# A ring of six weight units in which the low part overwrites the raw weight, with splits four units ahead

## The chip, the cores and the metric

One core of a Trainium2 chip runs one program: a transformer block with a mixed retention and neighbourhood attention, followed by two layers of a second kind of block. The metric is the device time of one execution in microseconds (us). Five engines take part: TensorE (PE) multiplies, VectorE (DVE) and ScalarE (ACT) do elementwise work, GpSimd (POOL) mostly issues DMAs, and the sync engine (SP) issues the DMAs of the weights. Each engine runs its instructions in order and waits on semaphores.

## The reference

```
x = x + 0.5 * rms(swiglu(rms(x) @ w_in) @ w_out)           # ffn1: 1024 -> 2 x 2816 -> 1024
x = x + rms(token_mixing(rms(x)))                          # w_mix_in 1024 x 6656, retention, attention, gates
x = x + 0.5 * rms(swiglu(...))                             # ffn2
mod = silu(c) @ ada_w + ada_b                              # 2 layers x 6 vectors of 1024
for i in range(2):                                         # layer 0: MoBA attention, layer 1: differential
    x = layer_norm(alpha * x + (1 + gate1) * attention(x * (1 + scale1) + shift1))
    x = layer_norm(alpha * x + (1 + gate2) * (relu(h @ w_up) ** 2) @ w_down)   # h = x * (1 + scale2) + shift2
```

There are 256 tokens of 1024 features, all in float32. The weights are read once, 198 MiB of them, so every weight is used for 256 tokens only.

## The kernel before

**Units.** All weights pass through a ring in units of 1 MiB, a tile of 128 x 2048 float32. There are 198 units (`N_UNITS`), numbered in the order in which PE uses them; unit u lies in slot u % `RING`. PE multiplies in the one-pass float32r format, and to keep precision each weight is split: ACT writes `hi_w`, the weight rounded to float32r (`split_hi`, L782), and DVE writes `lo_w = w_raw - hi_w` (`split_lo`, L1089). For each product PE then does three matmuls, hi x hi, lo x hi and hi x lo (`three`, L384 to L386), 24 matmuls of 512 columns in a unit. Activations are split alike into `xT_hi`, `xT_lo`, `hT_hi` and `hT_lo`.

**What sets the order.** SP issues the requests for units in order. Ahead of unit u it waits for `w_lo`, that is for the lo split of unit u - 4, which is the last reader of the raw slot (`slot_free`). ACT waits for the landing of unit u, and for PE to have used unit u - 4 (`w_used`), the last reader of `hi_w` and `lo_w` in that slot. DVE waits for `w_hi`. PE waits for `w_lo` ahead of a unit (`in_unit`, `down_unit`) and counts `w_used` after it. The splits are written into the programs of ACT and DVE by hand, between their other work, `AHEAD` = 3 units ahead of the unit that PE has in the same step.

**Start.** ACT and DVE split unit 0, then the first activations, then units 1 to `AHEAD` - 1 in a loop. After the loop ACT forms the squares of x (`x_squares`, L824) and `c_act` (L909), and DVE the factor of the norm (`x_factor`, L1119 to L1128), which the first SwiGLU activation needs. POOL waits for `w_lo` to reach `AHEAD` and then starts to fetch the weights of the adaLN modulation.

**SwiGLU blocks.** `swiglu` runs 11 blocks of 3 units: two units of gate and up projections, one of the down projection. PE does the gate and up units of block i + 1, transposing the hidden tile of block i between them (L429), then waits for `hT_lo` and does the down unit of block i. ACT has the activation (L840) and `hT_hi` (L847) between its splits, DVE the product (L1226) and `hT_lo` (L1183). In 8 of the 11 blocks of each SwiGLU, and in the first MLP, DVE also multiplies a piece of the adaLN weights by `c_act` (`piece_half` twice, four operations of L1194 and L1197 each, and `piece_fold`). A piece is two transfers of 1 MiB, one for each half, into a single buffer; POOL asks for each half of the next piece when DVE is through with that half (L1651). In block 1 of the first SwiGLU DVE has some 25 tiny operations more (`small_vectors`).

**Later stages.** The mixing stage, the two attentions and the two MLPs take units through the same ring. Between two stages PE waits while ACT and DVE form a norm.

Of the kernel before, what the change touches and what calls it, by code (L numbers as in the profile page):

```python
# [11 lines left out]
F32R = mybir.dt.float32r  # L12
# [3 lines left out]
P = 128  # L16
# [9 lines left out]
MLP_B = 512  # L26
N_MLP = D_MLP // MLP_B
UNIT = 2048
RING = 4
AHEAD = 3  # L30
RET_H, RET_DK, RET_DV = 4, 128, 256
NA_H, NA_D = 8, 64
GRID = 64
# [67 lines left out]
def ring_slot(u):  # L101
    return u % RING


def landed(u):
    return 32 * (u // RING + 1)

# [15 lines left out]
def two_blocks_kernel(nc, d, out):  # L123
    with ExitStack() as ctx:
        def sb(name, shape, dt=F32):
            return ctx.enter_context(nc.sbuf_tensor(name, shape, dt))

        def sem(name):
            return ctx.enter_context(nc.semaphore(name))


        w_raw = sb("w_raw", [P, RING, UNIT])
        hi_w = sb("hi_w", [P, RING, UNIT], F32R)
        lo_w = sb("lo_w", [P, RING, UNIT], F32R)
        x = sb("x", [P, NT, D])
        xT_hi = sb("xT_hi", [P, KD, SEQ], F32R)
        xT_lo = sb("xT_lo", [P, KD, SEQ], F32R)
# [92 lines left out]

        w_landed = [sem(f"w_landed{i}") for i in range(RING)]
        w_hi, w_lo, w_used = sem("w_hi"), sem("w_lo"), sem("w_used")
# [40 lines left out]
        def _(sp):  # L273
            def slot_free(u):

                if u >= RING:
                    sp.wait_ge(w_lo, u + 1 - RING)

            def unit(u, src, k):
                slot_free(u)  # L280
                dst = w_raw[:, ring_slot(u), :].rearrange("p (k n) -> p k n", k=k)
                sp.dma_start(dst, src).then_inc(w_landed[ring_slot(u)], 32)

            def swiglu_in(u, w, i, half):
                slot_free(u)
                dst = w_raw[:, ring_slot(u), :].rearrange("p (k g f) -> p k g f", k=4, g=2)
                for g in range(2):
                    src = w[:, 4 * half:4 * half + 4, g, i * FF_B:(i + 1) * FF_B]
                    sp.dma_start(dst[:, :, g, :], src).then_inc(w_landed[ring_slot(u)], 16)

            def swiglu(u0, w_in, w_out):
                w_in = w_in.rearrange("(k p) (g f) -> p k g f", p=P, g=2)
                w_out = w_out.rearrange("(b k p) n -> p b k n", p=P, k=2)

                def out_unit(u, i):
                    slot_free(u)
                    dst = w_raw[:, ring_slot(u), :].rearrange("p (k n) -> p k n", k=2)
                    src = w_out[:, i:i + 1, :, :].rearrange("p b k n -> p (b k) n")
                    sp.dma_start(dst, src).then_inc(w_landed[ring_slot(u)], 32)

                def step(u, i):
                    swiglu_in(u, w_in, i + 1, 0)
                    swiglu_in(u + 1, w_in, i + 1, 1)
                    out_unit(u + 2, i)

                swiglu_in(u0, w_in, 0, 0)
                swiglu_in(u0 + 1, w_in, 0, 1)
                for i in range(N_FF - 1):
                    step(u0 + 2 + 3 * i, i)
                out_unit(u0 + 3 * N_FF - 1, N_FF - 1)  # L310
# [46 lines left out]
            u = U_MIX + 2 * N_MIX  # L357
# [416 lines left out]
        def _(act):  # L774
            def split_hi(u):

                if u >= N_UNITS:
                    return
                act.wait_ge(w_landed[ring_slot(u)], landed(u))
                if u >= RING:  # L780
                    act.wait_ge(w_used, u + 1 - RING)
                act.activation(hi_w[:, ring_slot(u), :], w_raw[:, ring_slot(u), :], ACT.Copy).then_inc(w_hi, 1)  # L782

            def chunk_his(first, n, off, dst, dst0, scale=None):
# [48 lines left out]
            def swiglu(u0, b0, n, between=None):  # L833
                def activation(b, i):
                    act.wait_ge(w_used, u0 + 2 if i == 0 else u0 + 4 + 3 * (i - 1))
                    if i >= 1:
                        act.wait_ge(hid_done, b)
                    for t in range(NT):
                        pair = 4 + 2 * (i % 2)
                        ins = act.activation(act_s[:, t, 0:FF_B], ps[:, (pair + t) * BANK:(pair + t) * BANK + FF_B],  # L840
                                             ACT.Silu, scale=rstd_x[:, t:t + 1])
                    ins.then_inc(act_done, 1)

                def hidden_hi(b, i):
                    act.wait_ge(hidT, b + 1)
                    off = (4 + 2 * (i % 2)) * BANK
                    act.activation(hT_hi[:, 0:2, :], ps[:, off:off + 2 * SEQ].rearrange("p (c n) -> p c n", c=2),  # L847
                                   ACT.Copy).then_inc(hidT_hi, 1)

                split_hi(u0 + AHEAD)  # L850
                act.wait_ge(rstd_x_done, n)
                split_hi(u0 + AHEAD + 1)
                activation(b0, 0)
                for i in range(N_FF - 1):
                    u, b = u0 + 2 + 3 * i, b0 + i
                    split_hi(u + AHEAD)
                    hidden_hi(b, i)
                    split_hi(u + AHEAD + 1)
                    activation(b + 1, i + 1)
                    split_hi(u + AHEAD + 2)  # L860
                    if i == 1 and between is not None:
                        between()
                hidden_hi(b0 + N_FF - 1, N_FF - 1)
                split_hi(u0 + 3 * N_FF - 1 + AHEAD)

# [74 lines left out]
            u = U_MIX  # L940
# [830 lines left out]
```

## Time and profile before

| what | us |
|---|---|
| median of 3 runs | 1383.76 (1381.53 to 1384.84) |
| the profiled execution | 1381.94 |
| its span, first to last instruction | 1380.1 |
| PE busy | 1252.5 (91%) |
| DVE busy | 966.0 (70%) |
| ACT busy | 596.2 (43%) |
| POOL busy | 122.0 (9%) |

The span is what the trace covers; 1.8 us of the profiled execution's own time lie outside it. The profiled execution is 1.82 us quicker than the median of the three runs. Busy time counts an engine's instructions; matmuls overlap one another, so a busy PE is not PE at its peak. All times in the rows below count from the first instruction. The core moved 274.31 MB by DMA, of which 209.80 MB went through SP's queue and 63.56 MB through POOL's. The mean granted clock of TensorE was 0.954 of full speed.

### The profile page before, as it was taken

The numbers are of one execution on the slowest core, as the hardware profiler recorded it, in microseconds if no ns is written. First come the engines' busy times: TensorE is split into PE (matmuls) and PEld (weight loads), VectorE is DVE, ScalarE is ACT, GpSimd is POOL, SyncE is SP. The second block draws the span as 40 slices with busy tenths as digits, with TensorE's granted clock in tenths as the row PEclk, the third lists the DMA queues.
The fourth block names the chain that finished last, engine by engine and source line by source line (L and its number), as shares of the span: only waits on it lengthen the run. The fifth ranks groups of instructions, "written<-read, shape, count | busy, mean of one in ns | idle before, by whom it ended". The sixth has DMA issues, their size and how long they took to land.

```text
span 1380.1 us, 14621 instructions
## 1 busy us (share of the span) xinstructions
PE 1252.5 (91%) x5776; PEld 1027.9 (74%) x5776; DVE 966.0 (70%) x1244; ACT 596.2 (43%) x722; POOL 122.0 (9%) x148
## 2 busy tenths in 40 slices
PE   6999998999999899998899869999949975899995
PEld 5888876887888688887677647888738754688884
DVE  5998847765566698884756488878776876745454
ACT  5444444446653444444355334444334552434340
POOL 2000220004200000000000030001030001200000
PEclk9999998999999999999899789999979987999998
DMA  9989973535455599974543238787715330555520
GB/s 308 373 297 325 289 245 115 190 132 174 138 183 183 198 314 316 313 245 152 179 152 122 76 112 305 283 292 268 263 60 202 123 122 30 198 184 182 190 85 31
DMA packets 132596, 274.31 MB, mean 199 GB/s; under 512 B 6176, under 2 KB 51440, under 8 KB 132528
## 3 DMA queue, kind: packets, MB, share of 16 engines
q1 hardware_dynamic: 114672, 209.80, 44.5%
q0 software_dynamic: 17792, 63.56, 13.7%
q8 instruction: 46, 0.75, 0.2%
q14 instruction: 22, 0.18, 0.0%
q10 hardware_dynamic: 64, 0.02, 0.0%
HBM read 270.41 MB, written 2.93 MB: 198 GB/s over the span
## 4 chain that ended last, share of the span: by engine, by line
PE 77%; DVE 14%; ACT 3%; issue 3%; DMA 2%; SPq 0%; POOL 0%; DVEq 0%; ACTq 0%
PE ps L384 24%; PE ps L386 23%; PE ps L385 23%; PE ps L429 3%; DVE lo_w L1089 2%; DVE xT_lo L1110 1%; DMA w_raw<-in_ffn_w_in 1%; DVE piece_acc L1197 1%; DMA aux<-in_ada_w 1%; ACT area L1025 1%; DVE area L1517 1%; DVE xT_hi L1109 1%; PE ps L580 1%; DVE area L1142 1%; DVE x L1144 1%
## 5 line engine op out<-in xcount | busy, mean ns | idle before, releaser
L1089 DVE TENSOR_TENSOR lo_w<-w_raw,hi_w 128x2048 fp32r<-128x2048 f32 x198 | 454.3, 2300 | 175.1 <-ACT hi_w L782 174.7
L384 PE MATMUL ps<-hi_w,xT_hi 128*128 128x512 f32 x1120 | 453.0, 404 | 35.3 <-DVE xT_lo L1110 12.9
L782 ACT ACTIVATE hi_w<-w_raw 128x2048 fp32r<-128x2048 f32 x198 | 378.6, 1913 | 214.3 <-PE ps L386 203.1
L385 PE MATMUL ps<-hi_w,xT_lo 128*128 128x512 f32 x1120 | 442.2, 395 | 0.0
L386 PE MATMUL ps<-lo_w,xT_hi 128*128 128x512 f32 x1120 | 442.1, 395 | 0.0
L384 PEld LDWEIGHTS ps<-hi_w,xT_hi 128*128 128x128 f32 x1120 | 214.3, 191 | 85.2 <-issue 23.4
L386 PEld LDWEIGHTS ps<-lo_w,xT_hi 128*128 128x128 f32 x1120 | 213.9, 191 | 46.5
L385 PEld LDWEIGHTS ps<-hi_w,xT_lo 128*128 128x128 f32 x1120 | 214.8, 192 | 42.5
L384 PE MATMUL ps<-hi_w,hT_hi 128*128 128x512 f32 x464 | 182.2, 393 | 9.0 <-DVE hT_lo L1183 9.0
L386 PE MATMUL ps<-lo_w,hT_hi 128*128 128x512 f32 x464 | 181.2, 391 | 0.0
L385 PE MATMUL ps<-hi_w,hT_lo 128*128 128x512 f32 x464 | 181.2, 391 | 0.0
L384 PEld LDWEIGHTS ps<-hi_w,hT_hi 128*128 128x128 f32 x464 | 87.5, 189 | 28.8 <-DVE hT_lo L1183 10.9
L386 PEld LDWEIGHTS ps<-lo_w,hT_hi 128*128 128x128 f32 x464 | 87.5, 189 | 18.3
L385 PEld LDWEIGHTS ps<-hi_w,hT_lo 128*128 128x128 f32 x464 | 87.6, 189 | 18.0
L429 PE MATMUL ps<-ident,area 128*128 128x128 f32 x432 | 64.1, 295 | 31.6 <-ACT area L806 23.0
L429 PEld LDWEIGHTS ps<-ident,area 128*128 128x128 f32 x432 | 56.0, 153 | 42.0 <-ACT area L806 24.2
L1197 DVE SCALAR_TENSOR_TENSOR piece_acc<-aux,c_act,piece_acc 128x512 f32<-128x512 f32 x112 | 84.1, 751 | 4.1 <-DMA aux<-in_ada_w 0.6
L1183 DVE TENSOR_TENSOR hT_lo<-ps,hT_hi 128x512 fp32r<-128x512 f32 (+1 forms) x38 | 34.7, 913 | 58.1 <-ACT hT_hi L879 46.1
L847 ACT ACTIVATE hT_hi<-ps 128x512 fp32r<-128x512 f32 x22 | 13.2, 598 | 80.8 <-PE ps L429 80.8
L879 ACT ACTIVATE hT_hi<-ps 128x1024 fp32r<-128x1024 f32 x16 | 16.4, 1026 | 72.4 <-PE ps L429 72.4
L1025 ACT ACTIVATE area<-area,top 128x128 f32<-128x128 f32 x64 | 28.4, 444 | 40.3 <-DVE top L1521 30.4
L1651 POOL DMA_DIRECT2D aux<-in_ada_w x32 | 24.0, 750 | 237.2 <-DVE piece_acc L1197 206.2
(208 smaller groups left out, 912.9 us busy)
## 6 DMA issues: line engine op xcount, KB each, us to landing
w_raw<-in_ffn_w_in SPq DMA_DIRECT2D x88, 512.0 KB
aux<-in_ada_w POOLq DMA_DIRECT2D x32, 1024.0 KB, 7.2
w_raw<-in_mlp_w_up SPq DMA_DIRECT2D x32, 1024.0 KB
w_raw<-in_mlp_w_down SPq DMA_DIRECT2D x32, 1024.0 KB
w_raw<-in_w_mix_in SPq DMA_DIRECT2D x26, 1024.0 KB
w_raw<-in_ffn_w_out SPq DMA_DIRECT2D x22, 1024.0 KB
area<-in_ada_w POOLq DMA_DIRECT2D x16, 1024.0 KB, 5.7
w_raw<-in_moba_w_in SPq DMA_DIRECT2D x12, 1024.0 KB
```

The costliest lines, as they stand in the source:

```text
L384: pe.matmul(dst, lhs_hi, rhs_hi, start=start, stop=False)
L385: pe.matmul(dst, lhs_lo, rhs_hi, start=False, stop=False)
L386: return pe.matmul(dst, lhs_hi, rhs_lo, start=False, stop=stop)
L429: mm = pe.transpose(ps[:, off:off + P], src[:, t, col0 + c * P:col0 + (c + 1) * P], ident[:, :])
L580: mm = pe.matmul(ps[:, off:off + SEQ], nqT[row, h // 2, t * P:(t + 1) * P], nkT[row, h // 2, :], start=True, stop=True)
L782: act.activation(hi_w[:, ring_slot(u), :], w_raw[:, ring_slot(u), :], ACT.Copy).then_inc(w_hi, 1)
L879: act.activation(hT_hi[:, :, :], bank(pair, 2).rearrange("p (c n) -> p c n", c=4), ACT.Copy).then_inc(hidT_hi, 1)
L1025: ins = act.activation(pr, pr, ACT.Exp, bias=top[:, e, t:t + 1], accum_out=total[:, c % 2, 2 * e + t:2 * e + t + 1])
L1089: vec.tensor_tensor(lo_w[:, ring_slot(u), :], w_raw[:, ring_slot(u), :], hi_w[:, ring_slot(u), :].bitcast(F32), ALU.subtract).then_inc(w_l ...
L1183: vec.tensor_tensor(hT_lo[:, 0:chunks, :], src.rearrange("p (c n) -> p c n", c=chunks), hT_hi[:, 0:chunks, :].bitcast(F32), ALU.subtract). ...
L1197: ins = vec.scalar_tensor_tensor(out=acc, in0=row, scalar=c_act[:, c:c + 1], in1=acc, op0=ALU.mult, op1=ALU.add)
L1651: pool.dma_start(dst, ada[layer][:, 4 * half:4 * half + 4, i * BANK:(i + 1) * BANK])\
```

## The change

The ring becomes six units of two tensors instead of four units of three. `lo_w` is placed on the bytes of `w_raw`, so DVE's subtraction writes over its first operand. A raw slot is then in use until PE has used the unit, so SP waits for `w_used` of unit u - 6 ahead of its request for unit u. ACT's own wait for `w_used` goes, since a landed unit implies it. `AHEAD` is 4: each split in the programs of ACT and DVE is that of one unit later, the loops at the start hold unit 3 too, and POOL's first wait is for four lo splits.

```diff
-RING = 4
-AHEAD = 3
+RING = 6
+AHEAD = 4
...
+        w_base = (nc.sbuf_base + 31) // 32 * 32
         w_raw = sb("w_raw", [P, RING, UNIT])
+        lo_w = nc.alloc_sbuf_tensor_at("lo_w", [P, RING, UNIT], F32R, offset=w_base)
         hi_w = sb("hi_w", [P, RING, UNIT], F32R)
-        lo_w = sb("lo_w", [P, RING, UNIT], F32R)
...
             def slot_free(u):
                 if u >= RING:
-                    sp.wait_ge(w_lo, u + 1 - RING)
+                    sp.wait_ge(w_used, u + 1 - RING)
...
                 act.wait_ge(w_landed[ring_slot(u)], landed(u))
-                if u >= RING:
-                    act.wait_ge(w_used, u + 1 - RING)
                 act.activation(hi_w[:, ring_slot(u), :], w_raw[:, ring_slot(u), :], ACT.Copy).then_inc(w_hi, 1)
```

## Rows read from the trace of the kernel before

**Rows 1.** PE's waits: who waited for whom, us in total, times, longest.
```profile
PE ps L445 <- DVE x L1144: 18.7, 6, 5.8
PE ps L384 <- DVE hT_lo L1183: 9.0, 6, 2.4
```

**Rows 2.** The waits of ACT and DVE, and of SP's queue, same columns.
```profile
ACT hi_w L782 <- PE ps L386: 203.1, 63, 8.1
DVE lo_w L1089 <- ACT hi_w L782: 174.7, 96, 13.4
ACT hi_w L782 <- DMA w_raw<-in_ffn_w_in: 9.8, 3, 7.8
...
SPq L282 <- DVE lo_w L1089: 902.9, 132, 32.2
```

**Rows 3.** DVE's groups by shape: count | busy us, mean ns | idle before, releaser.
```profile
L1089 DVE TENSOR_TENSOR lo_w<-w_raw,hi_w 128x2048 fp32r<-128x2048 f32 x198 | 454.3, 2300 | 175.1 <-ACT hi_w L782 174.7
...
L1258 DVE TENSOR_TENSOR area<-area 128x1024 f32<-128x1024 f32 x16 | 19.6, 1223 | 13.8 <-ACT area L873 13.8
...
L1413 DVE TENSOR_TENSOR area<-area 128x1024 f32<-128x1024 f32 x2 | 2.5, 1226 | 0.0
```

**Rows 4.** The chain that ended last, first 80 us: start, us, what.
```profile
23.72 2.30 DVE lo_w L1089
...
26.30 0.76 POOL aux L1651
27.06 13.60 DMA aux<-in_ada_w
...
76.41 0.50 PE ps L384
```

**Rows 5.** Timeline of ACT at the start: start, us, operation [idle before <-releaser].
```profile
21.76 1.92 ACT L782 ACTIVATE hi_w<-w_raw 128x2048 fp32r<-128x2048 f32 x1 [0.78 <-DMA w_raw<-in_ffn_w_in]
23.59 1.04 ACT L824 ACTIVATE area<-x 128x1024 f32<-128x1024 f32 x1
...
27.19 3.71 ACT L782 ACTIVATE hi_w<-w_raw 128x2048 fp32r<-128x2048 f32 x2
30.80 0.81 ACT L840 ACTIVATE area<-ps,rstd_x 128x256 f32<-128x256 f32 x2
```

**Rows 6.** Timeline of DVE at the start.
```profile
33.61 0.87 DVE L1226 SCALAR_TENSOR_TENSOR area<-ps,rstd_x,area 128x256 f32<-128x256 f32 x2
...
39.35 0.68 DVE L1183 TENSOR_TENSOR hT_lo<-ps,hT_hi 128x512 fp32r<-128x512 f32 x1
40.68 3.12 DVE L1197 SCALAR_TENSOR_TENSOR piece_acc<-aux,c_act,piece_acc 128x512 f32<-128x512 f32 x4 [0.65 <-DMA aux<-in_ada_w]
```

**Rows 7.** Timelines of PE, ACT and DVE: first block, then a settled one.
```profile
36.02 0.60 PE L429 MATMUL ps<-ident,area 128*128 128x128 f32 x4
...
149.46 1.92 ACT L782 ACTIVATE hi_w<-w_raw 128x2048 fp32r<-128x2048 f32 x1 [2.85 <-PE ps L386]
...
166.25 1.92 ACT L782 ACTIVATE hi_w<-w_raw 128x2048 fp32r<-128x2048 f32 x1 [2.85 <-PE ps L386]
...
151.41 2.29 DVE L1089 TENSOR_TENSOR lo_w<-w_raw,hi_w 128x2048 fp32r<-128x2048 f32 x1 [1.61 <-ACT hi_w L782]
...
156.38 0.69 DVE L1183 TENSOR_TENSOR hT_lo<-ps,hT_hi 128x512 fp32r<-128x512 f32 x1
...
160.55 0.39 PE L384 MATMUL ps<-hi_w,hT_hi 128*128 128x512 f32 x1
```

**Rows 8.** Transfers: issues with median to landing, stretches (last columns PEclk, DMA, GB/s).
```profile
aux<-in_ada_w POOLq DMA_DIRECT2D x32, 1024.0 KB, 7.2
...
30.00:80.00 50.00, 49.30 (x224) 40.49 (x223) 47.52 (x71) 25.27 (x25) 4.07 (x6) 1.00 0.96 340
...
1225.39 5.85 SPq L282 DMA_DIRECT2D w_raw<-in_mlp_w_up  x2
...
1230.00:1231.00 1.00, 1.00 (x6) 0.85 (x5) 0.82 (x1) 0.00 (x0) 0.00 (x0) 1.00 0.02 8
```

## Prediction

> **What bounds the kernel now.** I read first what TensorE waited for. Its longest waits are for the norm of a finished stage, 18.7 us in 6 waits, with others of that kind; inside the stages it waits for the split hidden tile, `hT_lo`, 9.0 us in 6 waits [rows 1]. No wait of TensorE names `lo_w` or `hi_w`: it never waits for a weight unit after the first. Next the engines that prepare units. ACT idles 203.1 us ahead of `hi_w` because PE has not given a slot back, and 9.8 us for a landing; DVE idles 174.7 us for `hi_w`; the SP queue stands 902.9 us at L282 for `lo_w` [rows 2]. These are long, but they are the waits of engines that are ahead of the bound engine. So outside the boundaries and the attention chains the bound is PE's own work, and a deeper split lead can't pay there.
>
> One stretch is different. The chain of waits, cut to the first 80 us, is not PE's until 76.41: it goes from unit 2's lo split (23.72) to POOL's issue of the first adaLN pieces (26.30), through that transfer (27.06, 13.60 us), to the second piece half on DVE (40.68), and then along DVE until `hT_lo` releases PE at 76.41 [rows 4, 6]. Whatever enters this chain enters the time of the kernel. Everything after 76.41 is shifted with it.
>
> **The change, part by part.** The bytes of SBUF stay: 3 tensors of 4 units become 2 of 6. No matmul, split or transfer is added or removed (198 of each split [rows 3]).
>
> In place: DVE's 198 subtractions now write over their first operand. The trace has a same-size pair to compare, both 128x1024 f32: out of place (L1258) 1223 ns, in place (L1413) 1226 ns [rows 3]. That is 3 ns in 1223, at most 6 ns each on the 2300 ns of a split, 1.2 us in all on DVE, which is idle ahead of these splits 175.1 us [rows 3]. A gain has no reason, since shape and types are unchanged. I take 0. If the cover were gone it would be 1.2 us.
>
> ACT's dropped wait on `w_used`: the same release now stands in front of the request on SP. In the quiet up-and-down stage ACT was held by PE; now it is held by a landing. A request at 1225.39 has moved its bytes by 1230 (the window 1230 to 1231 moves 8 GB/s) [rows 8], so a landing takes about 5 us. The split in a given place of ACT's order is now that of the next unit, and its request leaves one unit earlier than ACT's old release: a PE unit is (166.25 - 149.46)/3 = 5.6 us, the same place of ACT's order three units apart [rows 7]. So the landing comes 5.6 - 5 = 0.6 us ahead of the old release. ACT gains up to 0.6 us that nobody waits for: 0. SP's wait on `w_used` has only later weight requests and the final store queued behind it; what a late landing does hold is ACT's next instruction, the hidden tile's `hT_hi`, and this is priced next.
>
> The loaded SwiGLU blocks: pieces of 1 MiB share the DMAs there, and the median of such a piece is 7.2 us [rows 8]; unit landings are not listed, so I take that row for them. Between 5 and 13.60 us [rows 4, 8] the 7.2 is nearest, being the same size in the same stage. The new place of 149.46 has its request at 143.9 and its landing at 151.1, 1.6 us late. DVE's lo split moves from 151.41 to 153.0, the four piece operations behind it likewise, and `hT_lo` from 156.38 (0.69 us long) to 158.0, ending at 158.7. PE takes it at 160.55 [rows 7]: 1.9 us of cover left. DVE's gap of 1.61 us ahead of its split takes the lateness up, so it does not grow from block to block. Cost 0; if the cover is gone, each us of landing beyond about 9.1 us is a us per block.
>
> The preamble is where AHEAD costs. Both `for u in range(1, AHEAD)` loops, ACT's and DVE's, now hold unit 3 as well, ahead of `x_squares` and `x_factor`; and `pool.wait_ge(w_lo, AHEAD)` now waits for unit 3's lo split. Unit 2 landed at 21.74 (ACT took it at 21.76 out of a wait for the DMA) [rows 5]; the requests are in one queue and the rate of the first full stretch is 340 GB/s [rows 8], so 1 MiB more is 3.1 us: unit 3 lands near 24.8. Then:
> - ACT: hi of unit 3 from 24.8 to 26.7, where `x_squares` began at 23.59 [rows 5]. Two squares, a table load and `c_act`, 3.6 us as before (23.59 to 27.19), end at 30.3; hi of units 4 and 5 end at 34.1; `activation` of block 0 starts there and not at 30.80. That is +3.3.
> - DVE: lo of unit 3 ends at 26.7 + 2.3 = 29.0, where lo of unit 2 ended at 26.0. `x_factor` ends near 31.0, lo of units 4 and 5 run from 32.3 to 36.8, and the product that began at 33.61 [rows 6] begins near 36.7: +3.1. PE reaches the transposes that need it at 36.02 [rows 7] and the product ends near 37.5, so PE stands 1.5 us. This is inside the delay below, not on top.
> - The next lo split, 4 piece operations and `hT_lo` follow; `hT_lo` was at 39.35 [rows 6] and comes at 42.4, ending at 43.1. PE is due there near 43.4. No stall.
> - POOL: its issue moves from 26.30 to 29.3, +3.0. The transfer took 13.60 us [rows 4], so the second half lands at 43.7 instead of 40.66. DVE is free for it at 43.1 (it used to stand 0.65 us for it [rows 6]).
>
> So DVE starts the second half between 2.4 us (its own order) and 3.0 us (landing) later. Nothing from there to 76.41 is idle except waits of well under a us, so PE resumes at 76.41 + 2.4 to 3.0. Could the next landings add? The unit whose split follows block 0 is requested when PE ends unit 3 (near 43.6) and needs to be in ACT's hands by about 51; at 7.2 us it is just there, at 8.4 us it adds 1.2: upper end 4.2. Below: if unit 3 landed with unit 2, hi would start at 23.7 and all is 1.1 us less: lower end 1.3.
>
> Which of 2.4 and 3.0? The row shows 13.60 us for 2 MiB behind the weights. The Trainium skill (DMA: Bandwidth & Descriptors, Queues, rings and completion order) says that a DMA engine takes the queue rows with work in turn, a packet of each. By that rule POOL's pieces get about half the rate however many weight requests stand in the other queue, so the transfer keeps its length when it starts later, and the result is the 3.0; if it were bytes in order of request, the same bytes would be through at 40.66 as before and DVE's own order would leave 2.4. Without the page I take the row's length unchanged: 3.0.
>
> The split lead inside the stages: one more unit split per unit of PE lead, same counts in each slot. The chain at the boundaries holds norms and chunk splits, no landing. Behind POOL's longer first wait stand only the pieces and later loads, whose other events are as before. 0. In the last stage one split fewer trails: nothing waits for it.
>
> **Sum.** Profiled run 1381.94 + 3.0 = 1384.9. That run is 1.8 below the median of the three, 1383.76; against the median 1386.8.
>
> **The rivals.**
> - *Start delay hidden* (0.22): the landing of unit 3 and of the pieces is quicker than bytes over rate, or requests of units 4 and 5 that leave earlier fill it. Then 0 to 2 us: 1384.8. For: units 4 and 5 no longer wait for lo splits. Against: the chain is DVE's work, which this does not shorten.
> - *Faster* (0.08): ACT freed of its 203.1 us [rows 2] hands over the in-stage tiles sooner and takes away part of PE's `hT_lo` waits, 9.0 us [rows 1]. Of these the ones at ends of stages are chains behind the last matmul, so about 3 us can go: 1380.8. Against: those tiles wait for PE's transposes, not for ACT.
> - *Slower by landings* (0.15): a six-slot ring asks for a unit only when PE has finished the sixth before it, where the old one asked after a lo split some 7 units ahead of PE. If loaded landings take over 9.1 us, each SwiGLU block with pieces stalls; at 10 us it is 0.9 us in 16 blocks, 14 us, with the start 1401. For: 13.60 for two pieces. Against: the 7.2 median. The Trainium skill (same page, Rules for kernel authors) advises to issue a DMA early and wait late; this change does the reverse for the raw units, and this rival is what the rule would cost here.
> - That the lead does nothing at all is no case of its own: it is the forecast without its 3.0, the first rival.
>
> **How the numbers follow.** Forecast 0.55. A measurement of this kernel tells about 0.2% (2.8 us) from no change. The forecast straddles that line: 1386.8 is 3.0 above, its ends 1.3 and 4.2; with about 1 us of spread in medians I give 0.37 of its 0.55 to slower, 0.18 to same. The first rival is all same, the second 0.07 faster and 0.01 same, the third slower. Slower 0.52, same 0.41, faster 0.07. Range: from 1383.0 (most of the hidden case in) to 1391.5 (the upper end, spread, and the mild cases of the landing rival); left out are the gain and the heavy landing cases.
>
> **What would show it.** In the changed profile: three splits become four ahead of the squares on ACT; the squares start near 26.6; POOL's first piece issue near 29.3; the product near 36.7; a PE wait of about 1.5 us near 37; the `hT_lo` wait at about 79 instead of 76.41. SP's waits name PE, no longer DVE; ACT's waits ahead of `hi_w` name DMA and are no shorter in sum than about 150 us; SwiGLU blocks still take 16.8 us. Blocks over 17 us, or PE waits on `lo_w`, would prove the landing rival; a missing shift of POOL's issue would prove the forecast wrong.

## The result and the profile after

The changed kernel takes 1399.05 us in the median (1396.28 to 1405.92, 4 runs), the kernel before 1383.66 (1381.53 to 1384.84, 4 runs): a ratio of 1.012, 95% interval 1.0081 to 1.016. By the ratio it is slower by some 16.6 us (0.012 x 1383.66; the two medians differ by 15.4), where 3.0 were forecast; the time lies beyond the range. The changed kernel scatters over 9.6 us in its 4 runs, the kernel before over 3.3 in these 4 and over 6.1 in 27 on another chip.

The profiled execution of the changed kernel has a span of 1398.4 us, 18.3 more than before. From its page come the busy times of the engines (us, share, instructions), the groups of the two splits (count | busy us, mean ns | idle before, releaser), and the transfers of the adaLN pieces (size, median us to landing; it was 7.2 [rows 8]):

```profile
PE 1258.1 (90%) x5776; PEld 1029.5 (74%) x5776; DVE 964.9 (69%) x1244; ACT 596.7 (43%) x722; POOL 123.0 (9%) x148
...
L1088 DVE TENSOR_TENSOR lo_w<-w_raw,hi_w 128x2048 fp32r<-128x2048 f32 x198 | 452.4, 2293 | 189.6 <-ACT hi_w L781 189.2
...
L781 ACT ACTIVATE hi_w<-w_raw 128x2048 fp32r<-128x2048 f32 x198 | 377.9, 1914 | 236.1 <-DMA w_raw<-in_ffn_w_in 103.2
...
aux<-in_ada_w POOLq DMA_DIRECT2D x32, 1024.0 KB, 7.7
```

The waits, the lines that answer to [rows 1, 2] (us in total, times, longest):

```profile
ACT hi_w L781 <- DMA w_raw<-in_ffn_w_in: 103.2, 22, 11.8
...
ACT hi_w L781 <- DMA w_raw<-in_mlp_w_down: 39.5, 15, 4.7
...
ACT hi_w L781 <- DMA w_raw<-in_mlp_w_up: 39.1, 10, 4.5
...
PE ps L385 <- DVE hT_lo L1182: 19.3, 10, 2.8
...
SPq L283 <- PE ps L387: 910.0, 132, 28.6
SPq L290 <- PE ps L387: 205.1, 39, 15.2
```

Three things are to be seen. First, the in-place split costs nothing: 2293 ns against 2300. Second, ACT's idle time ahead of `hi_w` is no shorter than before, 236.1 us against 214 (203.1 for PE and 9.8 for landings [rows 2]), and 234.6 of it are now waits for landings. Third, PE's waits for `hT_lo` went from 9.0 us in 6 [rows 1] to 19.3 us in 10. The 18.3 us divide so: 10.3 are these waits, 0.5 is a new wait for the first product, 0.7 the first transfer of x, which released PE at 7.20 instead of 6.52 (nothing that the change touches), and 5.6 are busy time of PE, 1258.1 against 1252.5 for the same 5776 matmuls. About 1.2 are spread over small gaps.

PE's busy time can grow only if matmuls get slower. The windows behind the new waits show it (columns as in [rows 8]: the granted clock PEclk is third from the end):

```profile
80.00:90.00 10.00, 10.00 (x39) 8.06 (x38) 9.86 (x11) 1.98 (x2) 0.75 (x1) 0.83 0.94 327
...
510.00:520.00 10.00, 8.17 (x37) 6.44 (x36) 9.79 (x11) 5.95 (x5) 1.50 (x2) 1.00 0.77 255
550.00:560.00 10.00, 8.57 (x31) 6.90 (x32) 9.84 (x12) 3.83 (x2) 1.50 (x2) 0.83 1.00 320
```

In both stretches of 0.83 PE ran some 3.4 us at 1.2 GHz in place of 2.4, which costs some 1.7 us each (0.17 x 10), 3.4 of the 5.6 us. The same stretch of the kernel before, 80 to 90, has 1.00. The other 2.2 us were not placed; the clock also falls at the ends of stages, in both kernels and not by the same amount. The 5.6 is itself rough: in the profiled executions of ring6_ahead3, ring6_ahead2, before_start4 and before_small_pieces (below), all within 0.1% of the kernel before, PE is busy for 1254.0, 1252.4, 1251.5 and 1251.0 us.

**One late landing, followed.** The chain of waits from 496 to 516, in the second SwiGLU (start, us, what):

```profile
496.83 10.52 DMA w_raw<-in_ffn_w_in
...
507.38 1.93 ACT hi_w L781
...
509.32 2.29 DVE lo_w L1088
511.62 0.41 DVE piece_acc L1193
...
512.05 0.76 DVE piece_acc L1196
...
512.84 0.76 DVE piece_acc L1196
...
513.62 0.75 DVE piece_acc L1196
514.37 0.61 DVE hT_lo L1182
...
515.03 0.50 PE ps L385
```

A landing releases ACT, ACT DVE, DVE does four piece operations and then `hT_lo`, and PE has been standing for it. The timelines give both ends of the landing. SP's queue and ACT, here and one such place later:

```profile
496.42 1.00 SPq L290 DMA_DIRECT2D w_raw<-in_ffn_w_in  x2
...
507.38 1.92 ACT L781 ACTIVATE hi_w<-w_raw 128x2048 fp32r<-128x2048 f32 x1 [8.30 <-DMA w_raw<-in_ffn_w_in]
...
532.15 1.57 SPq L290 DMA_DIRECT2D w_raw<-in_ffn_w_in  x2
...
543.77 1.92 ACT L781 ACTIVATE hi_w<-w_raw 128x2048 fp32r<-128x2048 f32 x1 [8.97 <-DMA w_raw<-in_ffn_w_in]
```

The units took 11.0 and 11.6 us from the first request to ACT. PE then waited 1.83 us at 515.03 and 2.50 us at 551.43. Take the 9.1 us at which the prediction put the end of the cover, that is the time that a landing may take before PE has to wait: 11.0 - 9.1 = 1.9 and 11.6 - 9.1 = 2.5. This limit was right to a tenth of a us; the landings were not 7.2.

The wait of 2.53 us at 185.25 has a longer landing behind it, and a longer cover. The chain there:

```profile
165.90 0.37 SPq L290
166.31 14.03 DMA w_raw<-in_ffn_w_in
180.36 1.93 ACT hi_w L781
182.31 2.29 DVE lo_w L1088
184.60 0.61 DVE hT_lo L1182
```

This block has no piece, so the four piece operations, 2.8 us at 511.62 above, do not stand between `lo_w` and `hT_lo`. From the request to ACT it is 14.5 us, and 14.5 - 9.1 - 2.8 = 2.6.

### The profile page after: what moved, and what is told of

Read it like the earlier page. It is cut to its first block, busy times and chain, and to the rows that moved or that the text cites. A ratio compares the mean times of both kernels' runs of the same rounds, so it can differ in the third digit from the quotient of the medians.

```text
span 1398.4 us, 14429 instructions
## 1 busy us (share of the span) xinstructions
PE 1258.1 (90%) x5776; PEld 1029.5 (74%) x5776; DVE 964.9 (69%) x1244; ACT 596.7 (43%) x722; POOL 123.0 (9%) x148
## 4 chain that ended last, share of the span: by engine, by line
PE 71%; DVE 15%; DMA 5%; ACT 4%; issue 3%; SPq 1%; DVEq 0%; ACTq 0%
PE ps L385 22%; PE ps L387 21%; PE ps L386 21%; DMA w_raw<-in_ffn_w_in 4%; PE ps L430 3%; DVE lo_w L1088 2%; DVE piece_acc L1196 2%; ACT hi_w L781 1%; DVE xT_lo L1109 1%; SPq L290 1%; ACT area L1024 1%; DVE area L1516 1%; DVE xT_hi L1108 1%; DMA w_raw<-in_diff_w_in 1%; PE ps L581 1%
## 5 line engine op out<-in xcount | busy, mean ns | idle before, releaser
L1088 DVE TENSOR_TENSOR lo_w<-w_raw,hi_w 128x2048 fp32r<-128x2048 f32 x198 | 452.4, 2293 | 189.6 <-ACT hi_w L781 189.2
L781 ACT ACTIVATE hi_w<-w_raw 128x2048 fp32r<-128x2048 f32 x198 | 377.9, 1914 | 236.1 <-DMA w_raw<-in_ffn_w_in 103.2
L385 PE MATMUL ps<-hi_w,hT_hi 128*128 128x512 f32 x464 | 184.9, 398 | 19.3 <-DVE hT_lo L1182 19.3
L386 PEld LDWEIGHTS ps<-hi_w,hT_lo 128*128 128x128 f32 x464 | 88.8, 191 | 18.3
L1196 DVE SCALAR_TENSOR_TENSOR piece_acc<-area,c_act,piece_acc 128x512 f32<-128x512 f32 x56 | 42.1, 751 | 1.8
```

The costliest lines, as they stand in the source:

```text
L385: pe.matmul(dst, lhs_hi, rhs_hi, start=start, stop=False)
L386: pe.matmul(dst, lhs_lo, rhs_hi, start=False, stop=False)
L1088: vec.tensor_tensor(lo_w[:, ring_slot(u), :], w_raw[:, ring_slot(u), :], hi_w[:, ring_slot(u), :].bitcast(F32), ALU.subtract).then_inc(w_l ...
L1196: ins = vec.scalar_tensor_tensor(out=acc, in0=row, scalar=c_act[:, c:c + 1], in1=acc, op0=ALU.mult, op1=ALU.add)
```

## The experiments

The theory: a request leaves when PE has finished unit u - RING, and the split of unit u stands where PE takes up unit u - AHEAD. Between them lie RING - AHEAD - 1 units of 5.6 us, called the distance here: 5.6 us in the changed kernel. A landing may take that and the slack of ACT and DVE, 9.1 us in all in a block with a piece. Most do not take more, but those beside two adaLN transfers of 1 MiB, or beside the bias table, sometimes do. A low granted clock follows some of the waits. The rivals: the in-place split or the new waits themselves cost the time; the deeper start costs more than 3 us; the low clock is chance.

Each ratio is against the kernel before on the same chip, with its 95% interval. The medians of the kernel before there were 1383.41 us (27 runs) for ring6_ahead3, before_start4 and the two with small pieces, 1383.09 (11 runs) for after_late_split, ring5_ahead3, ahead5 and after_small_late_table, and 1384.08 (17 runs) for the other four.

**ring6_ahead3**, the changed kernel with the old lead:

```diff
 RING = 6
-AHEAD = 4
+AHEAD = 3
```

> The changed kernel with AHEAD back at 3: ring of six, low part in place, SP waiting for PE, but each split is that of the unit three ahead. Theory (landings): a unit is requested when PE ends the sixth before it, and with AHEAD 3 its split stands one unit later in the orders of ACT and DVE, 5.6 us later, so even the landings of 10 to 12 us seen in the changed kernel come in time. And the loops at the start have three units again, so the start costs nothing. I expect 1383 to 1385, within 2 us of the kernel before. Rival (the ring itself costs, by the subtraction in place or by requests that follow PE): some 10 us or more of the 15 us stay, 1393 or higher.

Measured: 1383.57 us, ratio 0.999 (0.9981 to 0.9999). The ring of six, the split in place and the moved waits cost nothing together; all of the 16.6 us hangs on AHEAD. PE's wait of 0.70 us at 76.41 is gone too, and ACT's idle time ahead of its splits shrinks to 43.6 us. Long landings are still there; they are covered. Beside the bias table a unit that was requested at 156.30 reached ACT 17.3 us later, and PE waits for no `hT_lo` between 76 and 203:

```profile
156.30 11.80 SPq L290 DMA_DIRECT2D w_raw<-in_ffn_w_in  x4
...
173.65 1.92 ACT L781 ACTIVATE hi_w<-w_raw 128x2048 fp32r<-128x2048 f32 x1 [8.78 <-DMA w_raw<-in_ffn_w_in]
```

Here is ACT's group (columns as in [rows 3]), and below it those of three more kernels of the series:

```profile
L781 ACT ACTIVATE hi_w<-w_raw 128x2048 fp32r<-128x2048 f32 x198 | 373.5, 1913 | 43.6 <-DMA w_raw<-in_ffn_w_in 23.1 <-DMA w_raw<-in_mlp_w_down 9.1 <-DMA w_raw<-in_w_mix_out 7.1
```

ring6_ahead2:

```profile
L781 ACT ACTIVATE hi_w<-w_raw 128x2048 fp32r<-128x2048 f32 x198 | 371.7, 1914 | 15.4 <-DMA w_raw<-in_ffn_w_in 8.4 <-DMA w_raw<-in_ffn_w_out 4.1 <-DMA w_raw<-in_w_mix_out 1.6
```

ring5_ahead3:

```profile
L781 ACT ACTIVATE hi_w<-w_raw 128x2048 fp32r<-128x2048 f32 x198 | 377.9, 1915 | 243.4 <-DMA w_raw<-in_ffn_w_in 130.9 <-DMA w_raw<-in_mlp_w_down 77.7 <-DMA w_raw<-in_w_mix_out 8.6
```

ahead5:

```profile
L781 ACT ACTIVATE hi_w<-w_raw 128x2048 fp32r<-128x2048 f32 x198 | 379.0, 1914 | 639.3 <-DMA w_raw<-in_ffn_w_in 135.9 <-DMA w_raw<-in_ffn_w_out 123.1 <-DMA w_raw<-in_mlp_w_down 108.3
```

**ring5_ahead3**, a shorter ring and the old lead, the same distance as in the changed kernel:

```diff
-RING = 6
-AHEAD = 4
+RING = 5
+AHEAD = 3
```

> The changed kernel with a ring of five and splits three ahead. Theory: what decides is RING minus AHEAD, the units that PE uses up between a request and the place of its split in ACT's order; it is 2 here as in the changed kernel and 3 in ring6_ahead3. So PE's waits for the hidden tile in the loaded blocks are there again, some 9 to 13 us, while the start costs nothing: 1392 to 1397. Rival (a split lead of four is what hurts, by the order of work on DVE): within 2 us of the kernel before, since the lead is three.

Measured: 1397.14 us, ratio 1.0099 (1.0084 to 1.0114), as slow as the changed kernel although no split is added to its start. PE's waits for `hT_lo` sum to 19.9 us in 11; the longest, 2.90 us, does stand in the start, at 46.71, behind a unit that the shorter ring requests later. Not the lead and not the ring but their difference decides.

**ahead5**, the distance of nothing:

```diff
 RING = 6
-AHEAD = 4
+AHEAD = 5
```

> The changed kernel with splits five ahead in the ring of six. A split then stands one PE unit, 5.6 us, behind its request, and a quiet landing takes 5 us behind a request that itself comes late. Theory (RING minus AHEAD): now even landings of 7 us come late by 5 to 7 us in ACT's order, ahead of the hidden tile; each loaded SwiGLU block loses 2 to 4 us and the quiet ones little: 1425 to 1470. Rival (only rare late landings of over 10 us matter): 1405 to 1415.

Measured: 1492.13 us, ratio 1.0797 (1.0771 to 1.0822). The direction holds; the loss is beyond what was expected. Far more of each landing is now met, so ACT idles 639.3 us ahead of its splits, PE waits 56.7 us in 21 for `hT_lo`, and its busy time is 1292.1, 39.6 more than before. These two make 87 of the 109 us of the span; the others were not followed.

**ring6_ahead2**, a distance of three units, 16.8 us:

```diff
 RING = 6
-AHEAD = 4
+AHEAD = 2
```

> The changed kernel with a lead of two: a request leaves four units before its split. By the theory (only RING minus AHEAD counts, and three is enough) it is level with ring6_ahead3 and with the kernel before, within 0.1%, since two units of lead, 11 us, still cover ACT's and DVE's splits, 1.9 and 2.3 us. Rival (the splits need the lead of three against the work that ACT and DVE do at once at the ends of stages): PE waits for lo_w there, 5 to 20 us slower.

Measured: 1382.73 us, ratio 0.9994 (0.9984 to 1.0004). Even a lead of two units is enough, and a distance of more than two units brings nothing more. The series is then:

| RING, AHEAD | distance | ratio | ACT idle ahead of `hi_w` | PE's waits for `hT_lo` |
|---|---|---|---|---|
| 6, 2 | 16.8 us | 0.9994 | 15.4 | 8.3, 5 times |
| 6, 3 | 11.2 | 0.999 | 43.6 | 8.3, 5 |
| 5, 3 | 5.6 | 1.0099 | 243.4 | 19.9, 11 |
| 6, 4 (the change) | 5.6 | 1.012 | 236.1 | 19.3, 10 |
| 6, 5 | 0 | 1.0797 | 639.3 | 56.7, 21 |

**before_start4**, the start alone, put into the kernel before:

```diff
-                split_hi(u0 + AHEAD)
+                if u0 != U_FFN1:
+                    split_hi(u0 + AHEAD)
...
-            for u in range(1, AHEAD):
+            for u in range(1, 4):
                 split_hi(u)
...
-            pool.wait_ge(w_lo, AHEAD)
+            pool.wait_ge(w_lo, 4)
```

> The kernel before with one thing of the change: unit 3 is split in the loops ahead of the squares and of the norm's factor, and POOL's first wait is for four low splits. Ring of four, and from block 0 on the splits are three ahead as before. Theory (the start is a term of its own): DVE's chain to the first hidden tile that PE waits for is 2.4 to 3.2 us later, 1386 to 1387. In this kernel unit 3's split leaves its old place, so DVE's total work up to there is the same and only the order differs: if the cost is one more split of 2.3 us in DVE's busy chain, it is nearly 0 here; if it is the later start of the pieces' transfer and of the squares, it is up to 3.

Measured: 1385.04 us, ratio 1.0007 (0.9999 to 1.0016), 1.0 us more (-0.1 to 2.2). PE's wait that stood at 76.41 stands at 78.00:

```profile
78.00 0.50 PE L384 MATMUL ps<-hi_w,hT_hi 128*128 128x512 f32 x1 [1.57 <-DVE hT_lo L1184]
```

So in the old ring the start costs 1.0 us by the ratio and 1.6 by the place of this wait, not 3.0. Its requests at the start are not those of the changed kernel, and unit 3's split is only moved here, not followed by one more, so this does not settle what the start costs there.

**after_late_split**, the changed kernel with the extra split taken out of the start and put behind unit 13:

```diff
             def split_hi(u):
+                if u in (3, 14):
+                    return split_hi_of(13) or split_hi_of(14) if u == 14 else None
+                split_hi_of(u - 1 if 3 < u < 14 else u)
+
+            def split_hi_of(u):
...
-            pool.wait_ge(w_lo, AHEAD)
+            pool.wait_ge(w_lo, 3)
```

> The changed kernel, but up to block 3 of the first SwiGLU the splits are three ahead as before: the loops at the start hold units 1 and 2, POOL's first wait is for three low splits, and the one extra split is made behind that of unit 13. From there all is as in the changed kernel. Theory (the start and the landings are two terms that add): the wait near 77 shrinks to 0.7 us or less, 2.4 to 3.2 us go, with the stretch of low clock behind it up to 4.8; the waits at 180, 510, 550, 620 and 1005 stay. 1394 to 1397. Rival (the start's delay is made up later, or the landing waits come from where it shifted the pieces): 1399 as the changed kernel, or below 1390.

Measured: 1393.48 us, ratio 1.0077 (1.0062 to 1.0092). Some 6 of the 16.6 us go, and some 10 stay; the intervals of this kernel and of the changed one overlap a little, so the 6 is rough. In its profile the squares begin at 24.20, and the wait near 76 is 0.88 us long where the changed kernel has 2.21 at 79.61. With the 0.51 at 37 that is 1.8 us; another 1.7 are the low clock of 80 to 90, which is 1.00 here. The wait in the last blocks of the first SwiGLU is there still, 3.89 us at 182.09. What was expected of the second SwiGLU did not come: from there on the kernel is the changed one, and yet the waits of 1.83, 2.50 and 1.28 us are 0.23 us at 562.27 and 0.67 us at 613.67 in this execution, and 550 to 560 runs at 1.00. So not all of the 6 us can be put down to the start, and how late the landings are changes from one execution to another.

**after_small_pieces** and **before_small_pieces** take the bytes away from beside the units: of all adaLN pieces but the first of each group of eight only 64 of 512 columns are fetched. The modulation that comes of it is therefore not that of the reference; every instruction of the engines stays.

```diff
-                        pool.dma_start(dst, ada[layer][:, 4 * half:4 * half + 4, i * BANK:(i + 1) * BANK])\
+                        w = BANK if p == p0 else 64
+                        pool.dma_start(dst[:, :, 0:w], ada[layer][:, 4 * half:4 * half + 4, i * BANK:i * BANK + w])\
                             .then_inc(mod_landed[half], 16)
```

> The changed kernel, but of the adaLN pieces only the first of each group of eight is fetched whole; of the others only 64 of 512 columns are, 128 KB instead of 1 MiB a half, so the modulation is not computed rightly. DVE's operations stay the same. Theory (landings are late because pieces share the DMAs): a unit's landing stays near 5 us, the waits of PE for the hidden tile at 185, 515, 551, 621 and 1008 go, and with them the three stretches of lower granted clock that follow two of them; what is left is the start. 1385 to 1388, 2 to 4 above the next kernel. Rival (the stalls are from the order of ACT and DVE, not from DMA traffic): still 10 us or more above it.

> The kernel before with the same cut of the pieces' transfers, for comparison with the one above; the modulation is not computed rightly. It did not wait for landings after the first 40 us, so it stays at 1382 to 1384; up to 1 us may go at the start, where DVE stood 0.65 us for a piece.

Measured: 1392.49 us, ratio 1.0061 (1.0046 to 1.0077), and for the kernel before 1383.51, ratio 0.9999 (0.9988 to 1.0009). The pieces' bytes cost the kernel before nothing. The waits of the changed kernel at 515, 551 and 621 are gone without them: those landings were late because of the pieces. (In after_late_split they had nearly gone with the pieces whole, so pieces beside a unit make a late landing possible and not certain.) The time is above the 1385 to 1388 that were expected, for one wait remains, and it is longer than the one at 185 in the changed kernel:

```profile
187.33 0.80 PE L385 MATMUL ps<-hi_w,hT_hi 128*128 128x512 f32 x1 [7.36 <-DVE hT_lo L1182]
```

There POOL moves the table of the attention bias, after the last piece of the first SwiGLU. In the changed kernel the timelines of POOL and ACT show the transfer, and the landing beside it:

```profile
160.68 1.67 POOL L1664 DMA_DIRECT2D rel_scratch<-area  x1 [5.55 <-DMA area<-in_na_rel_bias]
178.26 0.55 POOL L1638 DMA_DIRECT2D aux<-in_mix_post_norm  x1 [15.91 <-DMA rel_scratch<-area]
...
180.36 1.92 ACT L781 ACTIVATE hi_w<-w_raw 128x2048 fp32r<-128x2048 f32 x1 [11.81 <-DMA w_raw<-in_ffn_w_in]
```

**after_small_late_table** is after_small_pieces with these transfers moved behind the first SwiGLU, and **after_late_table** is the changed kernel with that move alone:

```diff
-            pool.wait_ge(rel_zero, 1)
...
-            pool.wait_ge(rel_out, 16)
...
             pool.dma_start(rot1.rearrange("p c t n -> p (c t n)"), d["rot1"]).then_inc(ld_tab, 16)
+            pool.wait_ge(norm_done[1], S_FFN1 + 1)
+            pool.wait_ge(rel_zero, 1)
...
+            pool.wait_ge(rel_out, 16)
```

> after_small_pieces with one more edit: POOL's transfer of the bias table (1792 KB) and its loads wait for the end of the first SwiGLU. Of the pieces but the first of each eight only 64 of 512 columns are fetched, so the modulation is not computed rightly. Theory (landings are late because of what shares the DMAs, and in after_small_pieces the table's transfer made the one wait of 7.36 us at 187 and the lower clock behind it): those 10 us go and the start is left, 1384.5 to 1387. Rival (the wait at 187 is from the order of DVE's work in block 8): it stays, 1392.

> The changed kernel with the bias-table transfer of POOL moved behind the first SwiGLU, and nothing else. Theory (the table's transfer made the landing of 14 us at unit 30): the wait of 2.5 us near 185 goes, the waits in the second SwiGLU stay, and moving the table costs about 2 us in the mixing stage: 1395 to 1400, the same as the changed kernel within 0.3%. Rival (late landings come whatever else is on the DMAs there): a wait of over 2 us near 185 stays.

Measured: 1388.77 us, ratio 1.0044 (1.0031 to 1.0057), and 1396.23, ratio 1.009 (1.0069 to 1.0111). In both the wait near 185 is gone. In the second the waits of the second SwiGLU are there as before, 1.47, 3.14 and 1.09 us at 518, 555 and 625. In the first PE waits for `hT_lo` only 8.3 us in 5, as in ring6_ahead3: with the pieces small and the table later, PE waits for no late landing any more, and 6 of the 16.6 us are left. Somewhat more than expected; of these, some 4 are there by the end of the first SwiGLU (its last `hT_lo` wait at 205.48 against 201.61 in the kernel before), and the table itself makes PE wait some 2 us in the mixing stage. These 4 us are the nearest to a price of the start in the changed kernel's own ring, and they are not exact either: the first 50 us differ between executions of like programs. The granted clock is 0.96 and 0.87 from 30 to 50 here, worth some 1.6 us, and 0.76 from 20 to 30 in ring6_ahead3, where the profiled executions of the changed kernel and of the kernel before have 1.00. And the wait that the changed kernel has at 79.61 stands at 82.63 in after_late_table, whose start is the same program.

**stall_long** and **stall_short** measure what a wait costs beyond itself. They are ring6_ahead3 with 13 and 10 empty operations on DVE ahead of `hT_lo` in four blocks:

```diff
+                    if i in (3, 8):
+                        if piece is not None:
+                            vec.wait_ge(mod_step, KD * piece + 4)
+                        vec.wait_ge(hidT_hi, b + 1)
+                        for _ in range(13):
+                            then(vec.tensor_scalar(piece_acc[:, 0, :], piece_acc[:, 0, :], 1.0, None, ALU.mult))
                     hidden_lo(b, i, 2)
```

> The kernel before with a ring of six and a lead of three (level with before), and 13 empty operations on DVE, 0.51 us each as the 0.48 us multiplies of the pieces, ahead of hT_lo in 4 of the 22 SwiGLU blocks (blocks 3 and 8 of each SwiGLU). The cover there is 4.0 us, so PE should wait 4 times about 2.6 us, 10.4 us in all. Theory (a wait of 2.2 us or more is followed by a stretch of low granted clock, which costs again): the time grows by more than the waits, 13 to 17 us, and some of the four stretches behind a wait show a granted clock of 0.83. Rival (the low clock in the changed kernel came by chance, as it does in the kernel before): the time grows by the waits alone, 10 to 11 us.

> The same with 10 operations instead of 13: PE should wait 4 times about 1.1 us, 4.4 us in all. Theory: such short waits leave the granted clock at 1.00, the time grows by 4 to 5 us. Rival (each wait costs the clock something, however short): 6 us or more.

Measured: 1403.82 us, ratio 1.0142 (1.0129 to 1.0155), and 1396.28, ratio 1.0093 (1.0078 to 1.0107). The waits did not come out equal. PE's timeline of stall_long:

```profile
98.36 0.50 PE L385 MATMUL ps<-hi_w,hT_hi 128*128 128x512 f32 x1 [4.08 <-DVE hT_lo L1182]
189.84 0.80 PE L385 MATMUL ps<-hi_w,hT_hi 128*128 128x512 f32 x1 [5.57 <-DVE hT_lo L1182]
555.61 0.50 PE L385 MATMUL ps<-hi_w,hT_hi 128*128 128x512 f32 x1 [2.02 <-DVE hT_lo L1182]
643.50 0.50 PE L385 MATMUL ps<-hi_w,hT_hi 128*128 128x512 f32 x1 [1.93 <-DVE hT_lo L1182]
```

They sum to 13.6 us; stall_short has 2.82, 3.30, 0.63 and 0.54, together 7.3. The times grew by 0.0142 x 1384.08 = 19.7 us (17.9 to 21.5) and 12.9 us (10.8 to 14.8), 6 us more than these sums. But the waits are known in the profiled execution alone, and it was the quickest of each kernel. Taken by itself it is 1401.56 - 1384.08 = 17.5 and 1393.02 - 1384.08 = 8.9 us slower, so 3.9 and 1.6 us beyond its own waits. The other executions may have waited longer. That more than the waits is lost is borne out by the clock. Windows of stall_long:

```profile
100.00:110.00 10.00, 10.00 (x40) 8.16 (x39) 9.93 (x10) 0.00 (x0) 0.75 (x1) 0.86 0.59 212
...
190.00:200.00 10.00, 10.00 (x34) 8.06 (x35) 8.27 (x5) 1.91 (x1) 5.35 (x5) 0.76 0.38 107
550.00:560.00 10.00, 7.99 (x28) 6.10 (x28) 9.52 (x17) 5.01 (x5) 0.75 (x1) 0.84 0.84 287
640.00:650.00 10.00, 8.07 (x36) 6.33 (x36) 9.79 (x12) 4.44 (x4) 0.00 (x0) 1.00 0.34 107
```

The clock fell behind 4.08, 5.57 and 2.02 us and not behind 1.93. Windows of stall_short:

```profile
90.00:100.00 10.00, 7.18 (x28) 5.46 (x27) 9.50 (x17) 4.82 (x5) 1.44 (x2) 0.88 0.88 287
...
180.00:190.00 10.00, 6.70 (x23) 5.06 (x22) 9.65 (x16) 4.31 (x5) 0.85 (x1) 0.83 0.97 307
540.00:550.00 10.00, 9.37 (x44) 7.44 (x43) 7.87 (x16) 3.81 (x5) 0.75 (x1) 1.00 0.78 274
```

It fell behind 2.82 and 3.30 and not behind 0.63. The border that the theory drew at 2.2 us is not sharp: ring5_ahead3 has 0.83 from 120 to 130 behind a wait of 1.80 at 118.64, the changed kernel 1.00 behind one of 2.53 at 185.25. In ahead5 it is 1.00 behind one of 3.06 at 645.85. Nor is the low clock mere chance: in the profiled executions of the kernel before and of the four kernels level with it no stretch of 10 us between 50 and 200 or between 490 and 640 is below 1.00. What short waits alone would cost stays open, since two of the four were long.

## Why the prediction was wrong

The direction was right, the size was not; the mechanism that decides was named as the third rival, with a chance of 0.15 and a price of 14 us. The step that failed is the term for the loaded SwiGLU blocks, set at 0.

**In place, the dropped wait on ACT, the ring itself: 0.** Right. The split takes 2293 ns against 2300, and ring6_ahead3 is level with the kernel before.

**The start: +3.0.** Right in its places. The squares began at 26.71 (26.6 foretold), POOL's first piece was issued at 29.43 (29.3), the product began at 36.73 (36.7), PE waited for it near 37 (0.51 us, where 1.5 was foretold), and the wait for `hT_lo` stood at 79.61, 3.20 after 76.41 (about 79). From DVE's timeline of the changed kernel:

```profile
36.73 0.87 DVE L1225 SCALAR_TENSOR_TENSOR area<-ps,rstd_x,area 128x256 f32<-128x256 f32 x2
...
42.48 0.68 DVE L1182 TENSOR_TENSOR hT_lo<-ps,hT_hi 128x512 fp32r<-128x512 f32 x1
43.08 3.11 DVE L1196 SCALAR_TENSOR_TENSOR piece_acc<-aux,c_act,piece_acc 128x512 f32<-128x512 f32 x4
...
53.44 2.29 DVE L1088 TENSOR_TENSOR lo_w<-w_raw,hi_w 128x2048 fp32r<-128x2048 f32 x1 [0.73 <-ACT hi_w L781]
```

The choice between 2.4 and 3.0 went wrong: the second half of the piece starts at 43.08, without a wait, 2.4 us after its old 40.68. DVE's own order decided: the half issued at 30.19 landed at 40.54, before DVE was free for it. So the transfer did not keep its 13.60 us, as the forecast read out of the row of before. By the forecast's other reading, bytes in order of request, it would be there at 40.66 as before, and here it was. In before_start4 and after_late_table the same half landed at 42.10 and 43.23, so neither reading is shown in general. The forecast had drawn the first from the Trainium skill (DMA: Bandwidth & Descriptors, Queues, rings and completion order), which says that a DMA engine takes the queue rows with work in turn, a packet of each; this trace does not bear out the conclusion. The 0.73 us for a late landing at 53.44 is the "could the next landings add" of the forecast. 2.4 and 0.7 make the 3.1 or 3.2; PE's own lateness from x at the head, 0.7, is hidden in the wait, since DVE was later still. In time, before_start4 gives the start 1.0 us in the old ring and after_small_late_table some 4 in the new one; after_late_split is 6 quicker than the changed kernel, with the low clock behind the 2.21 us wait and some of the later waits in it. The forecast took that wait's delay and not the low clock behind it.

**The loaded SwiGLU blocks: 0.** This is the step that failed. It set the landing of a unit to 7.2 us, the median of the adaLN pieces, against a cover that ends at 9.1 us, and put the cost at 0. The cover was right, as the two waits of 1.83 and 2.50 us show; the landings behind them took 11.0 and 11.6 us, and 14.5 us beside the bias table, which the forecast did not look at. The landing was taken as one number where the cover is met in each of the 22 SwiGLU blocks. Most landings kept within it, for the changed kernel has four waits of over a us there, and the forecast of SwiGLU blocks of 16.8 us holds for the others. The four, 2.53, 1.83, 2.50 and 1.28 us, sum to 8.1. The row that warned was in the forecast: 13.60 us for two pieces behind the weights [rows 4], beyond the cover by 4.5. It served as the end of a range for the start and was not asked here how often something like it comes back. after_small_pieces and the two kernels with the later table show what it comes with: two pieces, or the table, in flight. The same sentence said that the lateness "does not grow from block to block"; that held.

**The clock: no term.** The forecast had none for what a wait does to the matmuls behind it. PE's busy time grew by 5.6 us, and the profiled executions of stall_long and stall_short lose 3.9 and 1.6 us beyond their waits. A term from the kernel before could have been had, since its stages end in waits of 5.8 us [rows 1] with a low granted clock behind them.

**The rivals.** *Start hidden* falls: before_start4 and the places above show the shift. *Faster* falls: ACT's 203.1 us went into waits for landings, 234.6 in sum over all units in the changed kernel, and PE's waits for `hT_lo` grew. *Slower by landings* is what happened, with 1401 in its sum and 1399.05 measured, though not as it was put: it priced 16 blocks at 0.9 us, and it was 4 blocks at 2, and the clock. That the two sums lie so near each other is luck. The whole series agrees with the Trainium skill's advice that it leaned on (DMA: Bandwidth & Descriptors, Rules for kernel authors: issue a DMA early, wait for it late): with 16.8 us of distance nothing is lost, with none 109 us are. Its chance should have been far higher, since the cover left was 1.9 us on a transfer that the same trace shows at 5, 7.2 and 13.60.

**Where the 16.6 us are.** Of the 18.3 us of the profiled execution's span the start is 3.2 (the shift of PE at 79.61), the four waits for late landings in the SwiGLUs 8.1, the slower matmuls 5.6, and a longer wait at the end of the first MLP 0.7 (2.85 us at 1008.79 where the kernel before waits 2.15). That is 17.6; 0.7 lie in small gaps. This is the account of one execution; other executions of the same program may divide otherwise.

**What stays open.** Why a landing beside two pieces takes 6 to 9 us most times and 10.4 to 11.6 in three of them was not found. The changed kernel's own scatter of 9.6 us and the small waits in the second SwiGLU of after_late_split suggest that it differs from run to run; each kernel has one trace. What the start costs in the changed kernel is known only as some 1 to 4 us.

## What to carry to other kernels

In a ring where the raw slot is held until the consumer is through, the time that a transfer has is (slots - lead - 1) units, so a longer lead takes time away from the transfers that it is meant to cover; write that distance down before changing either number. Compare it with the slowest landing the trace shows beside the same traffic, not with the median, and count how many times it is met. Price a wait of TensorE of two us or more in the middle of a dense stage above its length: the made waits cost 1.3 and 1.2 times theirs in the executions where they were measured (17.5 for 13.6, 8.9 for 7.3), the waits inside the SwiGLUs of the changed kernel 1.3 times (3.4 us of low clock on 10.4).

## What the runs showed of the hardware

In the middle of stages that otherwise run at 1.00 the granted clock fell to 0.76 to 0.88 over 10 us behind most waits of 1.8 to 5.6 us; it stayed at 1.00 behind waits of 0.54, 0.63, 1.83 and 1.93, once behind 2.53 and once behind 3.06. A 1 MiB weight landing that takes about 5 us in a quiet stage took 11.0 and 11.6 us beside two others of 1 MiB, and 14.5 and 17.3 us beside the write of the bias table. Removing most of the bytes of the adaLN stream left the kernel before where it was (0.9999) and took 0.6% off the changed one. A subtraction that writes over its first operand ran as fast as one that does not.
